# Second-layer loads moved, attention scores as plain float32 matmuls, and TensorE's three jobs of an attention step issued in alternating order

## The reference, cut to what matters

```
def stick_breaking(q, k, v, bias, q_offset):          # 8 heads of 64 channels
    z = einsum('bqhd,bkhd->bhqk', q * d ** -0.5, k) + bias
    causal = key_pos < qpos
    log_1mb = where(causal, log_sigmoid(-z), 0.0)
    excl    = (cumsum of log_1mb from the last key back, the key's own term left out)
    att     = where(causal, exp(log_sigmoid(z) + excl), 0.0)
    out     = einsum('bhqk,bkhd->bqhd', att, v)

x <- layer_norm(alpha * x + sublayer(x))              # after each layer
```

## Time and profile before

| | us |
|---|---|
| median of three executions | 3307.34 |
| the profiled execution | 3314.94 |
| its span, on which all rows are measured | 3313.2 |
| PE busy in it | 2906.6 (88%) |
| DVE busy | 2179.1 (66%) |
| ACT busy | 1262.2 (38%) |
| POOL busy | 826.0 (25%) |

### The profile page before, as it was taken

How to read it: one execution, slowest core, us unless ns; L and a number is a source line. 1 busy time by engine, 2 the same in 40 slices (tenths; PEclk the granted TensorE clock), 3 DMA queues, 4 the chain that set the end, 5 groups by cost and what they waited for, 6 DMA issues and landing times. The chain is left out here.

```text
span 3313.2 us, 70723 instructions
## 1 busy us (share of the span) xinstructions
PE 2906.6 (88%) x27987; PEld 2407.6 (73%) x27987; DVE 2179.1 (66%) x3338; ACT 1262.2 (38%) x2272; POOL 826.0 (25%) x726
## 2 busy tenths in 40 slices
PE   8799999977898958898799999979868988978698
PEld 7699999966776746676697877857646666658476
DVE  9526666547676637985358777613449899876587
ACT  1015555434444443342011011111128888864332
POOL 4100000012222322110211111112126676654221
PEclk9899999989999988998899999979989999999799
DMA  5524554464444555653559999963521101025542
GB/s 179 199 88 146 149 159 150 135 164 105 108 109 93 133 148 153 184 158 93 199 176 313 339 352 334 311 205 126 167 97 52 65 17 50 14 50 173 185 148 89
DMA packets 470755, 506.43 MB, mean 153 GB/s; under 512 B 200018, under 2 KB 363075, under 8 KB 465035
## 3 DMA queue, kind: packets, MB, share of 16 engines
q1 hardware_dynamic: 373466, 341.17, 34.1%
q10 hardware_dynamic: 88000, 143.93, 12.5%
q0 software_dynamic: 8960, 16.81, 1.8%
HBM read 360.68 MB, written 141.31 MB: 152 GB/s over the span
## 5 line engine op out<-in xcount | busy, mean ns | idle before, releaser
L2754 POOL TENSOR_TENSOR sp_att<-sp_beta,sp_left 128x512 f32<-128x512 f32 (+3 forms) x320 | 318.0, 1003 | 195.8 <-DVE sp_left L2710 184.1
L102 PE MATMUL po_acc<-po_x_high,po_w_low 128*128 128x412 f32 (+1 forms) x840 | 306.8, 365 | 36.9 <-POOL po_w_low L95 18.1
L102 PE MATMUL pe_acc<-pe_x_high,pe_w_low 128*128 128x412 f32 (+1 forms) x840 | 304.9, 363 | 22.4 <-DVE pe_x_low L95 14.8
L103 PE MATMUL po_acc<-po_x_low,po_w_high 128*128 128x412 f32 (+1 forms) x840 | 299.0, 356 | 0.0
L104 PE MATMUL po_acc<-po_x_high,po_w_high 128*128 128x412 f32 (+1 forms) x840 | 298.8, 356 | 0.0
L104 PE MATMUL pe_acc<-pe_x_high,pe_w_high 128*128 128x412 f32 (+1 forms) x840 | 295.7, 352 | 0.0
L103 PE MATMUL pe_acc<-pe_x_low,pe_w_high 128*128 128x412 f32 (+1 forms) x840 | 295.5, 352 | 0.0
L2710 DVE TENSOR_TENSOR_SCAN sp_left<-sp_z,sp_left,sp_zero 128x512 f32<-128x512 f32 x192 | 235.3, 1266 | 14.4 <-ACT sp_z L2654 12.6
L2441 DVE TENSOR_TENSOR po_work<-po_work,po_q 128x1024 f32<-128x1024 f32 x128 | 175.9, 1374 | 84.0 <-DMA po_work<-in_cache_k 78.3
L102 PEld LDWEIGHTS po_acc<-po_x_high,po_w_low 128*128 128x128 f32 x840 | 162.6, 194 | 85.2 <-ACT po_o L1183 31.5
L2646 ACT ACTIVATE sp_beta<-sp_z,sp_bias 128x512 f32<-128x512 f32 (+3 forms) x320 | 183.6, 631 | 72.7 <-PE sp_z L2585 44.8
(11 more groups left out here) (489 smaller groups left out, 7219.6 us busy)
## 6 DMA issues: line engine op xcount, KB each, us to landing
po_work<-in_cache_k SPq DMA_DIRECT2D x256, 256.0 KB, 5.1
po_work<-in_cache_v ACTq DMA_DIRECT2D x256, 256.0 KB, 4.7
scratch_ops<-pe_work SPq DMA_DIRECT2D x160, 128.0 KB, 2.1
out_z<-pe_o SPq DMA_DIRECT2D x84, 206.0 KB, 2.7
out_z<-po_o ACTq DMA_DIRECT2D x84, 206.0 KB, 4.6
pe_w<-in_w_e SPq DMA_DIRECT2D x21, 512.0 KB
po_w<-in_w_o ACTq DMA_DIRECT2D x21, 512.0 KB
rc_opx<-scratch_ops SPq DMA_DIRECT2D x16, 640.0 KB, 5.5
```

Source lines behind the costliest of these rows:

```text
L102: pe.matmul(out, ll, rh, start=start, stop=False)
L103: pe.matmul(out, lh, rl, start=False, stop=False)
L2754: pool.tensor_tensor(att[h][:, n % 3, 0:w], be[h][:, n % 4, 0:w], left[h][tile(n) % 2][:, at + 1:at + 1 + w], ALU.mult).then_inc(at_ok[h], 1)
```

## The change

It has these parts, all but the last about loads, their order and the work around them.

1. `rc`: the first load of operands is split in two with a semaphore each; one of POOL's DMAs stands earlier in its loop (`gpsimd_first`).
2. `oe`: y_b and its gate are loaded ahead of the weights, and ACT, DVE and POOL take the weights after the first gates. The sample tokens' state-space input becomes a few matmuls in place of broadcast products and sums on DVE. The units stand in other blocks.
3. `oe` and `oo`: LayerNorm's last part is two DVE operations instead of three.
4. `po`: ACT issues the weights of group 1 at its start and then of group i+2 at the opening of group i, one group earlier than before.
5. `pv`: the decay inputs come in one early load, q and k by column blocks, no longer unit by unit.
6. `sp`: scores are one float32 matmul per head; the splits of q and k on DVE go away; the first 512 columns of k and q are loaded first.
7. `oo`: squares and `back(0)` come ahead of the weight casts, and `back(1)` ahead of `tile(1)`.
8. `sp`: on PE the three jobs of a loop turn are issued in reverse order on odd turns.

```diff
@@ project_odd, ACT
             act.preload_act_table_set(LN_EXP)
+            pj.load_w(act, 1)
...
-                    if t in pj.opens and i + 1 < len(ODD_GROUPS):
-                        pj.load_w(act, i + 1)
+                    if t in pj.opens and i + 2 < len(ODD_GROUPS):
+                        pj.load_w(act, i + 2)
@@ Tail.tensor
-        tile(1, (0,))
-        centre(1)
-        glu(1)
-        tile(1, (1,))
-        back(1)
-        turned(0)
+        if self.even:
+            ...
+        else:
+            back(1)
+            tile(1)
@@ Tail.vector, norm
-            link(dve.tensor_scalar(y, y, self.mv[h][r, 0:1], self.sd[h][r, 1:2], ALU.subtract, ALU.mult))
-            link(dve.tensor_tensor(y, y, self.g[r, :], ALU.mult))
-            dve.tensor_tensor(y, y, self.b[r, :], ALU.add).then_inc(self.y_ok, 1)
+            link(dve.scalar_tensor_tensor(out=y, in0=y, scalar=self.mv[h][r, 0:1], in1=self.g[r, :], op0=ALU.subtract,
+                                          op1=ALU.mult))
+            dve.scalar_tensor_tensor(out=y, in0=y, scalar=self.sd[h][r, 1:2], in1=self.b[r, :], op0=ALU.mult,
+                                     op1=ALU.add).then_inc(self.y_ok, 1)
@@ project_values
-                sp.dma_start(ad[q][:, 0:width(n)], z[20, :, at]).then_inc(g_in[q], 16)
+            sp.dma_start(ad[:, :], z[20, 0:R_G, :]).then_inc(ad_in, 16)
@@ stick_prompt, scores
-                for t, (lhs, rhs) in enumerate(((ql, kh), (qh, kl), (qh, kh))):
-                    for h in (0, 1):
-                        r = slice(64 * h, 64 * h + 64)
-                        mm[h] = pe.matmul(zb[h][b][:, 0:w], lhs[q][r, cq].bitcast(F32R), rhs[q][r, ck].bitcast(F32R),
-                                          start=(t == 0), stop=(t == 2 and not diagonal(n)))
+                for h in (0, 1):
+                    r = slice(64 * h, 64 * h + 64)
+                    mm[h] = pe.matmul(zb[h][b][:, 0:w], qt[q][r, cq], kt[q][r, ck], start=True, stop=not diagonal(n))
@@ stick_prompt, PE's loop
             for n in range(N + FLIP + 1):
-                if n < N:
-                    scores(n)
-                if 0 <= n - FLIP < N:
-                    flip(n - FLIP)
-                if 0 <= n - FLIP - 1 < N:
-                    values(n - FLIP - 1)
+                work = ((scores, n), (flip, n - FLIP), (values, n - FLIP - 1))
+                for part, at in work if n % 2 == 0 else work[::-1]:
+                    if 0 <= at < N:
+                        part(at)
```

More of the change, by code:

```diff
@@ L631, in sync @@
                     (self.gw[:, :, :], self.const["glu_w"])]
-        for k in range(4):
-            weights(k)
+        if not self.even:
+            for k in range(4):
+                weights(k)
         for dst, src in maps:
@@ L636, in sync @@
         load_rest(0)
-        for k in range(4, KT):
+        for k in range(0 if self.even else 4, KT):
             weights(k)
@@ L785, in gpsimd @@
         weights(0)
-        weights(2)
-        weights(4)
+        if not self.even:
+            weights(2)
         low(0)
-        weights(6)
+        for k in ((2, 4, 6) if self.even else (4, 6)):
+            weights(k)
         for t in range(1, TT + 1):
@@ L848, in norm @@
             h, r = t % 2, slice(0, self.rows(t))
-            if t % 2 or t == 0:
+            if t % 2 or (t == 0 and self.even):
                 act.preload_act_table_set(LN_EXP)
@@ L872, in scalar @@
         act.wait_ge(self.eset, 2)
-        weights(0)
         squares(0)
-        for k in range(1, 4):
-            weights(k)
-        back(0)
-        gates(0)
-        act.wait_ge(self.cst_b, self.CST_B)
-        sigmoids(0)
-        for k in range(4, KT):
-            weights(k)
-        norm(0)
-        front(1)
-        put(0)
-        back(1)
-        put_turned(0)
+        back(0)
+        if not self.even:
+            for k in range(3):
+                weights(k)
+        act.wait_ge(self.cst_b, self.CST_B)
+        gates(0)
+        sigmoids(0)
+        for k in range(0 if self.even else 3, KT):
+            weights(k)
+        if self.even:
+            norm(0)
+            front(1)
+            put(0)
+            back(1)
+            put_turned(0)
+        else:
+            front(1)
+            back(1)
+            norm(0)
+            put(0)
         for b in range(1, self.NB):
@@ L1028, in vector @@
             unit(0)
+        else:
+            weights(1)
         gated(0)
         high(0)
-        weights(5)
-        weights(7)
+        for k in ((1, 3, 5, 7) if self.even else (3, 5, 7)):
+            weights(k)
         high(1)
         evict(0, 0)
-        evict(0, 1)
-        spread(0)
         if self.even:
+            evict(0, 1)
+            spread(0)
             centre(1, 0)
             centre(1, 1)
-        norm(0)
-        evict(1, 0)
-        if self.even:
+            norm(0)
+            evict(1, 0)
             unit(1)
-        scaled(1)
-        high(2)
-        next(samples, None)
+            scaled(1)
+            high(2)
+        else:
+            scaled(1)
+            evict(0, 1)
+            spread(0)
+            high(2)
+            norm(0)
+            evict(1, 0)
         for b in range(1, self.NB):
@@ L1067, in vector @@
             evict(t + 1, 0)
-            next(samples, None)
+            if self.even:
+                self.es.vector(dve, b)
         evict(TT - 1, 1)
```

331 lines of the change are left out of this document (179 added, 152 removed).

## The result

Four executions of the changed kernel took 3473.58 to 3482.63 us, median 3478.12; four of the kernel before, run beside them, had the median 3308.03. The ratio is 1.0508 with a 95% interval of 1.0481 to 1.0534: 5.1% slower. The forecast was 3392 us in a range of 3325 to 3460. The direction was right and the time lies outside the range. The profiled execution spans 3476.5 us against 3313.2, 163.3 more.

A forecast was written before the change was run, and what follows sets the result against it. The prediction took `sp` as the stage that matters most, with PE, ACT and DVE nearly full and DVE fullest. Alternating order +171, start of `sp` -7.5, other stages -78 gave +85 on 3307: 3392 us, range 3325 to 3460.

The forecast's parts named there:

- the loop: In `sp`, alternating order makes ACT and PE wait for each other through ACT's copy of step n-3, +171 us.
- 9.06 us for a full-width pair: In `sp`, predicted time of two full-width steps under the alternating order, against 6.24 us before.
- PEclk above 0.9: Sign in `sp` that the forecast was right: PE's granted clock stays above 0.9 through the stage.
- Where the clock fell before, the waits were 8 us and more: Argument that PE's clock would hold in `sp`, where PE idles about 2 us at a time.
- serial scores: Rival in `sp`: two heads' float32 scores run one after the other, +58 us, 3450; shares chance 0.12 with falling clock.
- The rival's working: In `sp`, PE's clock at the lower level for half the stage, +110, 3500 us; chance 0.12 shared with serial scores.
- its 670 us: Predicted length of the whole `sp` stage, against 498.5 us before; the sum was 676, less 6.
- Float32 scores: In `sp`, two heads' float32 matmuls run side by side, costing +0.1 to +0.17 us a step.
- The other stages: Waits removed and clock regained in `oe` -28, `po` -24, `pv` -11, `oo` -14, `rc` -1: sum -78 us.
- DVE loses 17 operations of 1.95 us, 33 us: In `oe`, DVE is left with some 215 of 354 us of work, so PE is the bound; stage -28 us.
- late load among the weights: In `oe`, weights that now come last may hold the first tile, losing up to 8 us of the gain.
- the 3 us of that part: In `oo`, the first rstd no longer waits for weight casts, -3 us of the stage's -14.

The follow-up runs named there:

- the fixed order: Changed kernel with PE issuing scores, transposes, values in that order on every turn of `sp`: 3232.70 us, ratio 0.9774 to the kernel before.
- the scores-first order: Changed kernel with scores first on every turn, only transposes and values changing places on odd turns: 3245.23 us, ratio 0.9798 to the kernel before.
- the two copies on ACT: Changed kernel with both heads' copies of the transposes on ACT, ahead of beta and keeps: 3321.74 us, ratio 1.0021 to the kernel before.
- ACT's copy first: Changed kernel with ACT's copy of transposes n-3 moved ahead of beta and keeps of step n: 3460.29 us, ratio 1.0452 to the kernel before.
- three with filled gaps: Changed kernel with unused PE matmuls added per pair of turns, 7 and 3, 7 and 1, 7 and 0: 3454.61, 3432.70, 3416.60 us.
- 7 and 0 products: Changed kernel with seven unused matmuls ahead of even turns' transposes and none ahead of odd turns' values: 3416.60 us, ratio 1.0317 to the kernel before.
- reversed on every turn: Changed kernel with values, transposes, scores in that order on every turn of `sp`, not every second: 3935.54 us, ratio 1.1885 to the kernel before.

## Why the prediction was wrong

**Right: the loop.** "values n-3, waits for ACT's copy of step n-3", and "there is a loop that only one of the two engines works in at a time". ACT waits 79 times, PE's values or their weight loads wait 79 times for ACT's copy (about 80 were forecast), and 9.06 us for a full-width pair came out at 8.98 at full clock. It is shown by the fixed order, the scores-first order and the two copies on ACT. One part was missing: DVE's copy closes a second loop, hidden behind the first, which only "ACT's copy first" brought out.

**Wrong: the clock.** The step that failed is the line "PEclk above 0.9", with "Where the clock fell before, the waits were 8 us and more". The forecast took the loop's price at full clock and gave a fallen clock a part of 0.12 among the rivals. It was at 0.85 over the stage, and between 0.80 and 0.90 in every 50 us from 2400 to 3100. With gaps filled the stage is 686.7 us, so 53 of the 70 us missed are the clock. It is somewhat more: that kernel had a few pairs below full clock too. With each pair's shortest time at full clock in the changed kernel or the three with filled gaps (the first two pairs, never at full clock, as they are), the 79 pairs come to some 664 us where the changed kernel has 722.7, and the clock to 59.

The premise didn't hold on the trace of before either. The earlier trace rows start from the largest waits and look at the clock around them; starting from the clock finds falls behind short ones. In `po` a single wait of 1.72 us stands in dense work, with 2 us of small products behind it (L2343, L2356), and the projection's matmuls then take 0.55 us where the one ahead took 0.35:

```profile
2050.95 0.35 PE L104 MATMUL po_acc<-po_x_high,po_w_high 128*128 128x412 f32 x1
2053.02 1.06 PE L2343 MATMUL po_sums<-po_work,po_att 128*8 128x512 f32 x8 [1.72 <-ACT po_att L2414]
...
2055.84 0.55 PE L104 MATMUL po_acc<-po_x_high,po_w_high 128*128 128x412 f32 x1
```

```profile
2054.00:2059.00 5.00, 5.00 (x25) 4.88 (x22) 2.44 (x2) 0.00 (x0) 0.00 (x0) 0.66 0.98 349
```

The clock fell in the same way behind waits of 1.25 us, with the same small products, at 1817.0 and 2172.3. The forecast had waits of about 2 us in every 9 and gave them a chance of 0.12, shared with serial scores. The rival's working, "PE's 224 us in the loop would grow by half, +110", took the lower level for half of the time; 0.85 is three tenths of the time, by which 110 becomes 66 us, near the 53 to 59 that the runs show. The price had been worked out; the chance given to it was far too low. The prediction cited the Trainium skill there for transposes. The same page of the Trainium skill (TensorE: Matmul & The Clock Gate, Part 1, "A second HAM failure mode") tells of a kernel whose clock swung because PE paused briefly and often between groups of matmuls. The runs here agree, 0.85 with pauses of 1 to 3 us, and that section was the one to weigh.

**The rest of the 70, 11 to 17 us.** Between the beta of step 1 and that of step 159 lie 79 pairs, for which the forecast had 661.6 of its 670 us. They take 670.7 with 7 and 0 products and some 664 by the shortest times above, so the forecast's loop was 2 to 9 us short. The other 16.0 us of the 686.7 are the stage's filling and draining, for which a sum of busy times had one pair's 8.4. That left 7.6 us out.

**Float32 scores: right, with a small size off.** The two heads overlap: 1.13 us for both, where one after the other would need 1.72 by the earlier trace rows. They cost 0.10 us a full-width step and not the 0.17 that the sum used; in the fixed order the stage with them is 2.9 us shorter, since the splits went. Serial scores, +58, did not happen. They have no share in the loss that a run could show.

**The other stages: right as a sum, not one by one.** 78.0 us for 85.5. `po`, `pv` and the start of `sp` came within 4 us. `oe` gave 12.3 and not 28. The step there was "DVE loses 17 operations of 1.95 us, 33 us", with some 215 us of work left. The three operations had 26.7, 31.9 and 19.6 us for 16 of each, 78.2; the two that replace them have 67.2, 11.0 us less, and DVE kept 240.6:

```profile
L1041 DVE SCALAR_TENSOR_TENSOR oe_y<-oe_y,oe_mean_var,oe_gain 128x1024 f32<-128x1024 f32 x16 | 34.7, 2168 | 6.1 <-ACT oe_std L874 5.0 <-DMA oe_shift<-in_ln_b 0.4
L1043 DVE SCALAR_TENSOR_TENSOR oe_y<-oe_y,oe_std,oe_shift 128x1024 f32<-128x1024 f32 x16 | 32.5, 2033 | 0.6
```

An operation was counted off and the greater length of the two that take over its work was not. The waits on PE in `oe` tell more (of those in the earlier trace rows, only the one of 10.1 us stands in the stretch where the forecast read DVE's 91%; the 7.0 is at 1296): the 10.1 and 9.6 us went, as did 7.8 on the gate of y_b, but the other gate, loaded behind them now, is waited for:

```profile
PE oe_part L687 <- DMA oe_gate<-out_z: 7.1, 1, 7.1
PE oe_part L713 <- DMA oe_gate<-out_z: 4.7, 1, 4.7
```

The forecast had looked for a late load among the weights. `rc` and the stages before it gave 12.7 for 1, of which the 9.3 in `rc` are clear of the spread. In `oo` the waits for rstd were 14.4 us in all and 14.1 before, the longest 10.6 and 12.7, so the 3 us of that part were 2 at most, given back in the others.

**The range** ended at 3460 for serial scores, a case that the trace spoke against, and stopped short of the fallen clock, 3500, a case to which the new gaps pointed.

**The version to keep** is the changed kernel with the fixed order: 3232.7 us, 2.3% faster than the kernel before and 7% faster than the changed one.

## What to carry to other kernels

When a reordering makes an engine wait for another engine's newest result, follow the queue of that other engine: what stands ahead of the awaited instruction, and what of it waits for the first engine. If the two close a ring, its length is the sum of both parts and no added depth shortens it; only the queue positions do, and each engine that carries a share of the result can close a ring of its own.

Then price the ring twice, once at full clock and once with TensorE's share stretched, because a ring leaves TensorE idle a few microseconds at a time all through the stage. To judge whether the clock will hold, look in the trace at hand for the shortest waits behind which it fell, not only at the longest ones.

Where operations are fused, subtract the old durations and add the new one's, even if it has to be bounded; a removed instruction is not its whole duration saved.

## What the runs showed of the hardware

- Gaps of 1 to 3 us, coming with every pair of turns, had PE's clock at 0.80 to 0.90 in each 50 us of the stage though PE was busy for 35 to 38 of them; a gap in every turn, 2.7 us on average, had it at 0.67. In `sp` before, such gaps were tenths of a microsecond and the clock 0.98. Matmuls whose results nobody uses, placed in the gaps, brought 0.98 to 0.99 and made the kernel faster: the stage by 53 us in the one order, by 266 in the other.
- In `po` of the kernel before a single wait of 1.72 us and 2 us of small products were followed by a clock of 0.66 over 2054 to 2059 us, with matmuls of 412 columns at 0.55 us in place of 0.35. Not every such gap does it: the changed kernel's pair at 2559.3 has waits of 2.23 and 0.63 us on PE and a clock of 1.00.
- Matmuls at the lower level are longer where they start late, and so lengthen the ring that made the gap: in "reversed on every turn" at least 266 of the 704 us over the fixed order are of that kind.
- A DVE operation with two tensors and a scalar took 2.03 to 2.17 us on average for 1024 columns (1.28 in the median), against 1.22 and 2.00 (median 1.22) for those with two tensors and 1.67 (0.81) for the one with a tensor and two scalars: of a fusion of three into two, 14% of the time remained as gain by the means and 21% by the medians (2.57 us for 3.26).
